# Attention of a two-block trunk kernel on one core: waits by PSUM bank, sums of later key chunks on VectorE, values of two heads in turn to two column groups

## The reference

```
z = einsum('bhqd,bhkd->bhqk', qb, kb) * scale
mask = s_pos < t_pos
log_keep = where(mask, log_sigmoid(-z), 0.0)
suffix = cumsum(log_keep, reverse=True) - log_keep
wts = where(mask, exp(log_sigmoid(z) + suffix), 0.0)
out = einsum('bhqk,bhkd->bhqd', wts, vb)
```

## Time and profile before

| | us |
|---|---|
| median of 3 runs | 1835.47 |
| lowest, highest | 1831.92, 1836.16 |
| span of the profiled execution, first to last instruction | 1824.3 |
| the profiled execution's own whole time | not recorded |
| busy in the span: TensorE, VectorE, ScalarE, GpSimd | 1705.0, 647.0, 443.7, 170.2 |
| mean granted clock of TensorE in the span | 0.969 |

### The profile page before, as it was taken

How to read it: one execution, slowest core, us unless ns; L and a number is a source line. 1 busy time by engine, 2 the same in 40 slices (tenths; PEclk the granted TensorE clock), 3 DMA queues, 4 the chain that set the end, 5 groups by cost and what they waited for, 6 DMA issues and landing times.

```text
span 1824.3 us, 21872 instructions
## 1 busy us (share of the span) xinstructions
PE 1705.0 (93%) x8774; PEld 885.3 (49%) x8774; DVE 647.0 (35%) x1210; ACT 443.7 (24%) x775; POOL 170.2 (9%) x172
## 2 busy tenths in 40 slices
PE   7999999889999999999699998999799999999983
PEld 3455564545445555455355548975433333333331
DVE  3379111242223122221269947542522221222213
ACT  2233552214312122111258512331100000000001
POOL 0000000011111111110000023100111111111110
PEclk9999999989999999999899999999799999999997
DMA  9274611389999999999480091044799999999994
GB/s 367 93 257 160 213 70 47 133 321 407 392 401 411 407 400 406 407 411 413 174 322 1 5 143 47 1 162 194 277 392 403 406 409 407 406 421 408 417 414 175
DMA packets 94220, 515.26 MB, mean 282 GB/s; under 512 B 22429, under 2 KB 28157, under 8 KB 69544
## 3 DMA queue, kind: packets, MB, share of 16 engines
q1 hardware_dynamic: 82920, 496.46, 70.0%
q0 software_dynamic: 11200, 17.39, 2.9%
HBM read 506.09 MB, written 27.05 MB: 292 GB/s over the span
## 4 chain that ended last, share of the span: by engine, by line
PE 70%; DMA 15%; issue 7%; DVE 5%; SPq 2%; ACT 1%; DVEq 0%; POOLq 0%
PE bank L852 22%; PE bank L868 10%; PE bank L454 8%; PE bank L462 8%; DMA ring<-in_w_up 7%; DMA ring<-in_w_down 4%; PE bank L809 3%; PE bank L839 3%; PE bank L730 2%; PE bank L879 2%; PE bank L520 2%; PE bank L685 2%; PE bank L447 1%; DVE arena L2549 1%; DMA ring<-diag 1%
## 5 line engine op out<-in xcount | busy, mean ns | idle before, releaser
L854 PE MATMUL bank<-ring,arena 128*64 128x512 f32 x928 | 418.7, 605 | 0.0
L852 PE MATMUL bank<-ring,arena 128*64 128x512 f32 x752 | 339.1, 604 | 9.4 <-DMA ring<-in_w_up 6.8
L868 PE MATMUL bank<-ring,arena 128*64 128x512 f32 x544 | 247.9, 598 | 2.6 <-DMA ring<-in_w_down 2.6
L870 PE MATMUL bank<-ring,arena 128*64 128x512 f32 x544 | 247.9, 598 | 0.0
L2448 DVE TENSOR_TENSOR arena<-arena,bank 64x512 f32<-64x512 f32 x70 | 48.3, 690 | 560.5 <-ACT arena L1763 560.5
L454 PE MATMUL bank<-arena,ring 128*128 128x512 f32 x560 | 244.6, 593 | 0.0
L852 PEld LDWEIGHTS bank<-ring,arena 128*64 128x64 f32 x752 | 100.7, 139 | 208.5 <-issue 202.4
L852 PE MATMUL bank<-arena 128*64 128x512 f32 x368 | 166.1, 605 | 9.3 <-DMA ring<-in_w_up 5.0
L1429 POOL DMA_INDIRECT arena<-xnd,smalli x70 | 67.6, 966 | 1074.4 <-PE bank L839 536.0
L454 PEld LDWEIGHTS bank<-arena,ring 128*128 128x128 f32 x560 | 105.2, 190 | 127.2 <-issue 127.2
L1763 ACT ACTIVATE arena<-bank 64x512 f32<-64x512 f32 x70 | 41.2, 588 | 512.1 <-PE bank L854 512.1
(11 more groups left out here) (439 smaller groups left out, 1999.2 us busy)
## 6 DMA issues: line engine op xcount, KB each, us to landing
ring<-in_w_down SPq DMA_DIRECT2D x62, 2048.0 KB, 33.2
ring<-in_w_up SPq DMA_DIRECT2D x54, 2048.0 KB, 16.9
ring<-in_w_gate SPq DMA_DIRECT2D x45, 2048.0 KB, 17.4
arena<-in_w_gate SPq DMA_DIRECT2D x19, 2048.0 KB, 25.2
ring<-in_w_mod SPq DMA_DIRECT2D x12, 2048.0 KB, 8.0
ring<-in_w_in SPq DMA_DIRECT2D x10, 2048.0 KB, 15.7
arena<-in_w_up SPq DMA_DIRECT2D x10, 2048.0 KB, 29.8
ring<-in_w_out SPq DMA_DIRECT2D x4, 2048.0 KB
```

Source lines behind the costliest of these rows:

```text
L852: pe.matmul(GU[0:CAP, :], x, wg_[:, c, :], start=(c == 0), stop=(c == KD - 1), skip_group_check=True)
L854: mm = pe.matmul(GU[CAP:2 * CAP, :], x, wu_[:, c, :], start=(c == 0), stop=(c == KD - 1), skip_group_check=True)
L868: pe.matmul(Y[0:CAP, :], x, wd_[:, c, 0:512], start=(c == 0), stop=(c == 3), skip_group_check=True)
L870: mm = pe.matmul(Y[CAP:2 * CAP, :], x, wd_[:, c, 512:1024], start=(c == 0), stop=(c == 3), skip_group_check=True)
```

## The change

Six edits, all in the attention:

- scores go bank by bank in the order bank 2 (chunk 2), bank 1 (chunks 1 and 3), bank 0: product, then mask, then an increment of z_ready. The waits on w_raw are by bank as well.
- softplus goes by bank too: Abs, Exp and Ln of a bank are three instructions, interleaved over the banks.
- scored does bank 2, bank 1, bank 0, each as its Ln is ready. Behind bank 1 VectorE makes three 128-column sums of softplus of later chunks (`below`).
- decays is nine matmuls in three groups by bank; chunks 2 and 3 for chunk 1's and chunk 0's queries come as one sum from `below`. arg_ready counts three a head.
- values is issued once for a pair of heads, the two heads' matmuls of a chunk in turn; o_ready counts pairs.
- TensorE's order is decays(2p), scores(2p+2), decays(2p+1), scores(2p+3), values(p).

```diff
+        PIECES = ((2, 256, (2,)), (1, 512, (1, 3)), (0, 512, (0,)))
+        below = [area(5, 3072 + 384 * i, 384) for i in range(2)]
...
             def scores(h):
                 z = zbanks[h % 2]
-                if h >= 2:
-                    pe.wait_ge(S("w_raw"), 3 * (h - 1))
                 r = HD * (h % 2)
-                for c in (0, 1, 3, 2):
-                    pe.matmul(zpart(z, c), qk[r:r + HD, 4 + h // 2, P * c:P * c + P],
-                              qk[r:r + HD, h // 2, P * c:T], start=(c != 3), stop=False,
-                              skip_group_check=True)
-                for c in range(4):
-                    mm = pe.matmul(zpart(z, c)[:, 0:P], M["ident"], far, start=False, stop=True,
-                                   skip_group_check=True)
-                mm.then_inc(S("z_ready"), 1)
+                for i, (bank, width, held) in enumerate(PIECES):
+                    if h >= 2:
+                        pe.wait_ge(S("w_raw"), 3 * (h - 2) + i + 1)
+                    for c in held:
+                        mm = pe.matmul(zpart(z, c), qk[r:r + HD, 4 + h // 2, P * c:P * c + P],
+                                       qk[r:r + HD, h // 2, P * c:T], start=(c != 3), stop=False,
+                                       skip_group_check=True)
+                    for c in held:
+                        mm = pe.matmul(zpart(z, c)[:, 0:P], M["ident"], far, start=False, stop=True,
+                                       skip_group_check=True)
+                    mm.then_inc(S("z_ready"), 1)
 
             def decays(h):
...
+                z, sp, bl = zbanks[h % 2], spb[h % 2], below[h % 2]
+
+                def less(c, q0, q1, mat, src, last):
+                    return pe.matmul(zpart(z, c)[:, P * (q0 - c):P * (q1 - c)], mat, src, start=False, stop=last,
+                                     skip_group_check=True)
+
+                pe.wait_ge(S("sp_raw"), 3 * h + 2)
+                less(2, 2, 4, M["nge"], kpart(sp, 2), False)
+                less(2, 3, 4, M["nones"], kpart(sp, 3), True).then_inc(S("arg_ready"), 1)
+                less(3, 3, 4, M["nge"], kpart(sp, 3), True)
+                less(1, 1, 4, M["nge"], kpart(sp, 1), False)
+                less(1, 2, 3, M["nones"], kpart(sp, 2)[:, 0:P], True)
+                pe.wait_ge(S("below"), 3 * h + 1)
+                less(1, 3, 4, M["nones"], bl[:, 2 * P:3 * P], True).then_inc(S("arg_ready"), 1)
+                pe.wait_ge(S("sp_raw"), 3 * h + 3)
+                less(0, 0, 4, M["nge"], kpart(sp, 0), False)
+                less(0, 1, 2, M["nones"], kpart(sp, 1)[:, 0:P], True)
+                pe.wait_ge(S("below"), 3 * h + 3)
+                less(0, 2, 4, M["nones"], bl[:, 0:2 * P], True).then_inc(S("arg_ready"), 1)
+
+            def values(p):
+                o = psum[6 + p % 2]
+                pe.wait_ge(S("w_raw"), 3 * (2 * p + 2))
+                if p >= 2:
+                    pe.wait_ge(S("o_taken"), p - 1)
+                if p == 1:
                     pe.wait_ge(S("root_c"), 1)
                 for c in range(4):
-                    mm = pe.matmul(o[r:r + HD, P * c:T], vtok[:, c, HD * h:HD * h + HD], kpart(wb[h % 2], c),
-                                   start=(c == 0), stop=(c == 3), skip_group_check=True)
+                    for i in range(2):
+                        h, r = 2 * p + i, HD * i
+                        mm = pe.matmul(o[r:r + HD, P * c:T], vtok[:, c, HD * h:HD * h + HD], kpart(wb[i], c),
+                                       start=(c == 0), stop=(c == 3), skip_group_check=True)
                 mm.then_inc(S("o_ready"), 1)
...
-            for h in range(NH):
-                decays(h)
-                if h:
-                    values(h - 1)
-                if h + 2 < NH:
-                    scores(h + 2)
-            values(NH - 1)
+            for p in range(NH // 2):
+                for h in (2 * p, 2 * p + 1):
+                    decays(h)
+                    if h + 2 < NH:
+                        scores(h + 2)
+                values(p)
...
-            sp.wait_ge(S("z_ready"), NH)
+            sp.wait_ge(S("z_ready"), 3 * NH)
...
             def softplus(h):
...
+                absolute(0)
+                exponential(0)
+                absolute(1)
+                logarithm(0)
+                exponential(1)
+                absolute(2)
+                logarithm(1)
+                exponential(2)
+                logarithm(2)
...
-                act.wait_ge(S("arg_ready"), h + 1)
                 if h >= 2:
-                    act.wait_ge(S("o_ready"), h - 1)
-                for b, w in ((0, 512), (1, 512), (2, 256)):
-                    A(wb[h % 2][:, 512 * b:512 * b + w], z[b][:, 0:w], ACT.Exp).then_inc(S("w_raw"), 1)
+                    act.wait_ge(S("o_ready"), h // 2)
+                for i, (bank, width, _) in enumerate(PIECES):
+                    act.wait_ge(S("arg_ready"), 3 * h + i + 1)
+                    A(wb[h % 2][:, 512 * bank:512 * bank + width], z[bank][:, 0:width], ACT.Exp).then_inc(S("w_raw"), 1)
...
             def scored(h):
...
+                for i, (bank, width, _) in enumerate(PIECES):
+                    s_ = slice(512 * bank, 512 * bank + width)
+                    dve.wait_ge(S("ln_ready"), 3 * h + i + 1)
+                    STT(sp[:, s_], z[bank][:, 0:width], 0.0, lnb[:, s_], ALU.max, ALU.add).then_inc(S("sp_raw"), 1)
+                    if i == 1:
+                        dve.wait_ge(S("sp_raw"), 3 * h + 2)
+                        TTo(bl[:, 2 * P:3 * P], kpart(sp, 2)[:, P:2 * P], kpart(sp, 3), ALU.add).then_inc(S("below"), 1)
+                        TTo(bl[:, 0:P], kpart(sp, 1)[:, P:2 * P], kpart(sp, 2)[:, 0:P], ALU.add).then_inc(S("below"), 1)
+                        dve.wait_ge(S("below"), 3 * h + 1)
+                        TTo(bl[:, P:2 * P], kpart(sp, 1)[:, 2 * P:3 * P], bl[:, 2 * P:3 * P], ALU.add)\
+                            .then_inc(S("below"), 1)
```

More of the change, by code:

```diff
@@ L722, in scores @@
-                mm.then_inc(S("z_ready"), 1)
-            def decays(h):
[L726 to L741, removed]
+                for i, (bank, width, held) in enumerate(PIECES):
[9 more added lines that the diff above has]
+                    mm.then_inc(S("z_ready"), 1)
@@ L1698, in softplus, with part, marked, absolute @@
                 z = zbanks[h % 2]
-                act.wait_ge(S("z_ready"), h + 1)
-                if h:
-                    act.wait_ge(S("sp_raw"), 3 * h)
-                for b, w in ((0, 512), (1, 512), (2, 256)):
[L1703 to L1706, removed]
+                def part(i):
+                    bank, width, _ = PIECES[i]
+                    return lnb[:, 512 * bank:512 * bank + width], z[bank][:, 0:width]
+                at = {}
+                def marked(ins, name):
+                    chained[0] += 1
+                    ins.then_inc(S("act_chain"), 1)
+                    at[name] = chained[0]
+                def absolute(i):
+                    act.wait_ge(S("z_ready"), 3 * h + i + 1)
+                    if h:
+                        act.wait_ge(S("sp_raw"), 3 * (h - 1) + i + 1)
+                    marked(A(part(i)[0], part(i)[1], ACT.Abs), f"abs{i}")
+                def exponential(i):
+                    act.wait_ge(S("act_chain"), at[f"abs{i}"])
+                    marked(A(part(i)[0], part(i)[0], ACT.Exp, scale=-1.0), f"exp{i}")
+                def logarithm(i):
+                    act.wait_ge(S("act_chain"), at[f"exp{i}"])
+                    A(part(i)[0], part(i)[0], ACT.Ln, bias=one).then_inc(S("ln_ready"), 1)
+                absolute(0)
[7 more added lines that the diff above has]
+                logarithm(2)
             def squared(p):
@@ L2219, in scored @@
             def scored(h):
-                z = zbanks[h % 2]
-                dve.wait_ge(S("ln_ready"), h + 1)
+                z, sp, bl = zbanks[h % 2], spb[h % 2], below[h % 2]
                 if h >= 2:
[L2223 to L2226, removed]
+                    dve.wait_ge(S("arg_ready"), 3 * (h - 1))
+                for i, (bank, width, _) in enumerate(PIECES):
[9 more added lines that the diff above has]
+                            .then_inc(S("below"), 1)
             def taken(p):
-                dve.wait_ge(S("o_ready"), 2 * p + 2)
+                dve.wait_ge(S("o_ready"), p + 1)
                 CP(yA[:, p, :], psum[6 + p % 2][:, :]).then_inc(S("o_taken"), 1)
+            dve.wait_ge(C.full, C.at("pw1"))
             scored(0)
```

## The result

The kernel after takes 1819.6 us (median of 4 runs, 1815.9 to 1825.2) against 1835.4 (4 runs): ratio 0.992, interval 0.990 to 0.994, 15.7 us less. I had forecast 1825.0, in 1821.0 to 1829.5. The way and the place are right, the gain is larger than the range allows. Two timed runs of before, of 80 in this study, took 2243.8 and 2944.5 us at mean clocks of 0.742 and 0.553; no ratio or median here counts them. The profiled execution has a span of 1814.1 us and took 1815.9 in all, so what lies around the span is 1.8 us and not 11.2. VectorE's waits in this stage show none for it.

A forecast was written before the change was run, and what follows sets the result against it. TensorE was taken to bound the attention, at 10.08 us a head. Eight heads -9.0, start -2.3 and end +0.8 gave -10.5 us, so 1835.5 would become 1825.0 us, range 1821 to 1829.5.

The forecast's parts named there:

- Decays: TensorE, per head: nine matmuls with 2048 columns instead of ten with 2560, 3.47 us against 4.34, so -0.87.
- Values: TensorE: two heads' passes in turn overlap fully, 2.50 us a pair with shape changes, 1.25 a head against 2.30, so -1.05.
- The rule that the prediction weighed against the rows: Weight loads overlap matmuls only where row groups differ; would add 1.1 us a pair, making the sum -6.1 us; not followed.
- no overlap at all: Values: the opposite extreme to full overlap, nothing gained; as a rival, column groups don't overlap, 1833.6 us, chance 0.06.
- the sum: Whole kernel: -9.0 us for eight heads, -2.3 at the start, +0.8 at the end, together -10.5 us.
- Scores: TensorE, per head: going bank by bank makes six tile shape changes instead of two, 4 x 0.20 = +0.80 us.
- Start: TensorE's waits for the first STT results (0.64 us) and first weights' Exp (1.45 us), with weight loads, vanish: -2.3 us.
- End: The last values, values(3), wait for head 7's last Exp, 0.59 us plus some 0.2 for handovers: +0.8 us.
- ScalarE's order: Exp of head h+1 stands behind softplus(h+2); slack some 0.6 to 0.9 us on every other head, cost 0 if starts overlap.
- the rival (0.14): ScalarE is late by its order in the attention: gain only 6 to 8.5 us, 1827 to 1829.5 us; chance 0.14.
- The stages behind: Expert stage starts earlier by the attention's gain, which stays; rival, gain given back through clock levels, 1831 us, chance 0.05.
- the distance from span to median: Profiled span 1824.3 us to median run 1835.5: 11.2 us, taken as unchanged by the change.

The follow-up runs named there:

- masks first: Kernel after with a head's masks for all three banks issued before the products of all three; attention 70.0 us, ratio to before 0.992.
- Masks last: Kernel after with all products of a head issued first, then all its masks; attention 72.5 us, ratio to before 0.993.
- waits by head: Kernel before with nine-matmul decays, VectorE sums, paired values and new TensorE order, but waits and softplus per whole head; attention 89.9 us, ratio 1.001.

## Why the prediction missed

Step by step:

- **Decays** -0.87 a head: right, 4.34 to 3.49, and 6.8 us for eight heads when undone.
- **Values** -1.05 a head: right, 2.30 a pair. The rule that the prediction weighed against the rows, from the Trainium skill ("TensorE: Matmul & The Clock Gate", Part 3, The mechanism), would have made a pair 2.30 + 1.1 = 3.4 us, which the 2.30 measured contradict. What I had wrong is the other end, "no overlap at all": issued head by head a pair takes 3.86 us and not 2 x 2.15 + 0.15 = 4.45, so 0.59 overlap by themselves, and undoing the turns costs 6.2 us and not the 8.6 I expected. As the last pair of before had this overlap already, its values shorten by less than the sum has it, some 0.4 us of the stage (estimate from the pieces of the two chains).
- **Scores** +0.80 a head for four more changes of shape: right, 3.44 to 4.22, and with two changes again (masks first) 3.53. The added increments cost nothing that the rows show.
- **Start** -2.3: in the profiles compared this stands. The first score to the first decays takes 10.2 us instead of 9.2, with the longer scores and no wait, and there is none behind it. **This is the term that was mis-sized.** I priced the waits as bare idle time, 2.3 us. In two of three profiles of before the granted clock fell behind them, for 1.6 and 3.3 us more; in none of after, which has no such waits. So the waits cost 2.3, 3.9 and 5.6 us in the three profiles, and on average the change saves 85.8 - 73.9 = 11.9 us of attention and not 10.5. That the same waits brought the clock down in two profiles and not in the third has no cause that the runs show; the profile I had read was the one without.
- **End** +0.8: right, 0.7.
- **ScalarE's order**: the slack was there, and thin as said; the rival (0.14) did not come true for the kernel after. Masks last is the case where it is gone.
- **The stages behind** kept the gain: the 573.7 us from the projection's first matmul on, with the experts, are the same in both kernels (286.3 to 860 and 277.5 to 851.2). What lies outside the attention differs no more between the kernels than between executions of one.

The sum for the profiled pair was -10.5 and came out at -10.3 for the attention, -10.2 for the span. The rest of the distance to -15.7 has two parts. One is the 1.4 us more on the average of three profiles. The other, and the larger, is luck: over all timed runs of both kernels in this study before has a median of 1833.3 (78 runs) and after of 1821.5 (17 runs), 11.8 us less, which is what three profiles each give for the attention. The first four runs of each lay 2.1 above the one and 1.8 below the other. Against 1821.5 the forecast would have stood inside its range, at its edge. Where the spread from run to run arises was not settled; the three profiles of after agree in the attention to 0.1 us and differ by 7 us in the span.

The range was therefore the second mistake: single runs spread with 4 us (standard deviation, before) and 3.6 us (after), so medians of four carry some 2 us each, an estimate (the deviation over the root of four), and a lower end of 4 us under the forecast had to hold that and a term never priced. The forecast also took the distance from span to median, 11.2 us, for something that lies around the span. It is 1.8; the other 9.4 us say that the profiled execution was faster than the median run, a sign that its profile might not show what the median run does. As the forecast only subtracts the gain from the median, this error didn't move it.

## What to carry to other kernels

A wait ahead of TensorE is worth more than its length where it brings the granted clock down, and whether it does can differ from one execution to the next. So price it at its idle time, and as a bound at the next passes at half speed, and look at more than one profile of the kernel before. Less work with waits in it can be slower than more work without: with waits by head the stage took 89.9 us in the one profile taken, and 81.1 with 10.3 us of useless work in the gaps. Where tile shapes alternate, order the work so that the shape changes seldom but the first result still comes early: masks first, then products by bank, did both.

## What the runs showed of the hardware that I had not expected

- With idle stretches of 1.45 to 2.43 us ahead of six heads' scores (waits by head), TensorE's clock was at its 1.2 GHz level for part of the stage: 0.89 on average, 0.66 over ten us. Behind the two waits of before's start (0.64 and 1.45 us) it fell in two profiles of three and not in the third. With idle stretches of 0.80 to 1.38 us (masks last) it stayed at 1.00 in one profile, and so it did where filler took the place of most of the idle time.
- Two column groups overlap even when one group's matmuls are all ahead of the other's in the list: two 512-column passes of the second head ran beside the first head's last ones, 0.59 us saved a pair.
- A change of tile shape between 64x128 and 128x128 costs 0.20 us either way (the pieces of scores: 0.63, 0.42, 1.06), one from 128x64 back 0.19 (3.68 for 3.49), one into it 0.15. The Trainium skill ("TensorEngine Tiling (Array Packing)", Key Properties) has it that changing the mode drains the engine. The rows agree in that each change costs time; they don't show what the time goes into.
- The distance between a run's time and its span was 1.8 to 1.9 us in all runs whose time is known.
